# One core, two transformer blocks: a bank wait split in two, three short chains moved, and evacuations spread over the chunks of the next group

## The chip, the cores and the metric

The kernel is one program on one core of one Trainium2 chip. Its five engines run their own instruction lists and meet through semaphores: PE (TensorE, with PEld for its weight loads), DVE (VectorE), ACT (ScalarE), POOL (GpSimd, hardly used here) and SP (SyncE, which issues the DMAs). The metric is the device time of one execution in microseconds (us), lower is better.

## The reference

Two blocks of two layers each run one after the other on 256 rows of width 1024, all in float32. The first block mixes four kinds of attention; the second has an mLSTM layer and an MLA layer, each with a gated convolutional feed-forward. What the change touches is inside these lines:

```python
# first block, each layer (attention = 28 "units" of the kernel)
proj = h @ w_in[layer]                     # q, k, v of all mixers, gates of the NSA heads
kc = gelu(blocks_of(k_c) @ wk1) @ wk2      # compressed keys, values alike; one short chain
g = sigmoid(gates); lam = exp(..) - exp(..) + lambda_init
# second block, mLSTM input: 256 latent and 256 context rows together
x_m = h @ w_up                             # 1024 -> 2048
x_c = silu(dwconv3(x_m, conv_w, conv_b))   # depthwise, 3 taps along the sequence
# second block, feed-forward (ffn(0): 512 rows, ffn(1): 256 rows)
gate, up = split(h @ w_in, 2)              # 1024 -> 2 x 2816
y = (silu(dwconv3(gate, conv_w, conv_b)) * up) @ w_out
```

## The kernel before

**Linears.** Every large product goes through one stream of *groups*. A group is a set of four output tiles of 128 columns (four "tickets", one PSUM bank of 512 float32 columns each; there are 8 banks), accumulated over K = 8 *chunks* of 128 input rows. Each operand is split in a high part in `fp32r`, a copy made by ACT, and a low part, a subtraction made by DVE. PE then multiplies high by high, high by low and low by high, so a chunk of four tickets is 12 matmuls of 128x512 (L758). Input parts lie in `xs` (ACT L1262, DVE L1717), which has room for two chunks of 512 columns: ACT can make the high part of chunk k when PE has done chunk k-2. Weight parts lie in `ws` (ACT L1238, DVE L1692) and come from 1 MB slots of a ring of two that SP fills; a slot holds four chunks, and its split is two operations of 128x1024 on either engine. `feed_to(q)` puts the splits for chunk q on an engine's list; behind chunks 1 and 5 of such a group it adds the split of the next weight slot. PE waits for a chunk's low part, the last of its operands.

**Evacuation.** When a group is done, its banks are emptied while the next group is multiplied. The Python loop `for k in range(KD)` calls `feed_to(nxt.q0 + k)` and then whatever was hung on that k, so the table of k values is the order on ACT and DVE. In the loop of `m_up` (16 tickets, four groups) a ticket p costs ACT the centre tap of the convolution (`centre_tap`, L1453), a copy of the bank (L1470) and later SiLU (L1474), and costs DVE the two outer taps (`outer_taps`, L1965 and L1967). In `ffn(0)` (11 groups of two gate and two up tickets) a pair p costs ACT one centre tap and two copies (L1588, L1591) and later SiLU (L1596), and costs DVE the outer taps and later the product of gate and up (L2210). In the loop of group 1 ACT also scales the residual at k = 6 and 7 (L1449, L1445). SiLU needs another table on ACT than what runs before, so its first use loads it (ACT_TABLE_LOAD).

**First block.** After the linears `proj` and `nat` of a layer, ACT and DVE empty their banks (ACT L1340, L1343, L1344 for `nat`); PE transposes a hidden row of the compression MLP into the bank `hidT` (L918), and then goes through the units: scores `S` of unit i (L952, L953), one modulation product `ada` (L967), the transposes of the probabilities of unit i-2 or so (L1009) and the output `O` of unit i-3 (L1028). Before unit 0 PE waits until all 8 banks from before `hidT` are free. DVE empties `hidT` (L1820), makes the argument of the gelu (L1824 to L1830), then the lambda and the gates (L1832 to L1840), and only then adds the bias to the logits of unit 0 (L1867, L1869). ACT makes the exponential of the gelu (L1354) ahead of its loop, DVE ends the gelu at i = 1 (L1847 to L1851).

Of the kernel before, what the change touches and what calls it, by code (L numbers as in the profile page):

```python
# [391 lines left out]
def build(nc, tokens, stream, side, params, params1, consts, onehot, out, scratch):  # L392
    with ExitStack() as ctx:
# [330 lines left out]
        def _(pe):  # L724
# [156 lines left out]
            for l in range(DEPTH):  # L881
# [39 lines left out]
                for n in range(N(("hidT", l)) - BANKS + 1, N(("hidT", l)) + 1):  # L921
                    pe.wait_ge(bank_free[n % BANKS], n // BANKS + 1)
                for i in range(NU + 3):
# [72 lines left out]
                    if 0 <= i - 2 < NU:  # L996
# [216 lines left out]
        def _(act_):  # L1213
# [349 lines left out]
            def ffn(l, lo):  # L1563

                groups, per = ((NFF // 2, 2), (6, 4))[l]
                for i in range(groups + 1):
# [4 lines left out]
                    start = int(l == 0 and not last)  # L1571
                    for k in range(KD):
# [19 lines left out]
                        if 2 <= k < 2 + before:  # L1592
                            j = per * (i - 1) + k - 2
# [82 lines left out]
        def _(dve):  # L1676
# [85 lines left out]
            for l in range(DEPTH):  # L1762
# [55 lines left out]
                n = N(("hidT", l))  # L1818
                dve.wait_ge(bank_full[n % BANKS], n // BANKS + 1)
                v.tensor_copy(hid.rearrange("p a b -> p (a b)"), ps(n, 0, 64)).then_inc(bank_free[n % BANKS], 1)  # L1820
                dve.wait_ge(bank_free[n % BANKS], n // BANKS + 1)

                gx = lamp.rearrange("p (a b) -> p a b", a=4)
                v.tensor_tensor(gx, hid, hid[:, :, 15:16].to_broadcast([P, 4, 16]), ALU.add).then_inc(dve_own, 1)  # L1824
                dve.wait_ge(dve_own, own(dve_own))
                v.tensor_tensor(hidg, gx, gx, ALU.mult).then_inc(dve_own, 1)
                dve.wait_ge(dve_own, own(dve_own))
                v.tensor_scalar(hidg, hidg, 0.044715, 1.0, ALU.mult, ALU.add).then_inc(dve_own, 1)
                dve.wait_ge(dve_own, own(dve_own))
                v.tensor_tensor(hidg, hidg, gx, ALU.mult).then_inc(gelu_arg, 1)  # L1830
                dve.wait_ge(lam_exp, seen(lam_exp))
                v.tensor_tensor(lam[:, 4:5], lam[:, 3:4], lam[:, 2:3], ALU.subtract)  # L1832
                v.tensor_scalar(lam[:, 6:7], par_at(("subln", l)), 1.0 - lam_init, None, ALU.mult).then_inc(dve_own, 1)
                dve.wait_ge(dve_own, own(dve_own))
                v.tensor_scalar(lam[:, 5:6], lam[:, 4:5], -lam_init, None, ALU.add)

                dve.wait_ge(gate_exp, seen(gate_exp))
                v.tensor_scalar(lam[:, 16:40], lam[:, 16:40], 1.0, None, ALU.add).then_inc(dve_own, 1)
                dve.wait_ge(dve_own, own(dve_own))
                v.reciprocal(lam[:, 16:40], lam[:, 16:40]).then_inc(dve_own, 1)  # L1840
# [631 lines left out]
```

## Time and profile before

| what | value |
|---|---|
| median of three executions | 2338.24 us (2337.72, 2338.24, 2345.36) |
| the profiled execution's own time | 2337.17 us |
| span of the profiled execution | 2335.3 us, mean granted clock 0.996 |
| PE, PEld, DVE, ACT busy | 96%, 80%, 58%, 51% |
| stretch of `m_up` groups 1 to 3 | 793.50 to 865.20 us |
| stretch of `ffn(0)` groups 1 to 10 | 1565.16 to 1793.28 us |
| first unit of layers 1 and 2 | 89.82 and 463.90 us |

The profiled execution took 1.9 us more than its span, and 1.07 us less than the median. All times of the trace count from the start of the span. A line of the timeline gives the start, the duration, the engine, the source line, the operation, what it writes and reads, and in brackets how long the engine was idle before it and whose end it waited for.

### The profile page before, as it was taken

The numbers are of one execution on the slowest core, as the hardware profiler recorded it, in microseconds if no ns is written. First come the engines' busy times: TensorE is split into PE (matmuls) and PEld (weight loads), VectorE is DVE, ScalarE is ACT, GpSimd is POOL, SyncE is SP. The second block draws the span as 40 slices with busy tenths as digits, with TensorE's granted clock in tenths as the row PEclk, the third lists the DMA queues.
The fourth block names the chain that finished last, engine by engine and source line by source line (L and its number), as shares of the span: only waits on it lengthen the run. The fifth ranks groups of instructions, "written<-read, shape, count | busy, mean of one in ns | idle before, by whom it ended". The sixth has DMA issues, their size and how long they took to land.

```text
span 2335.3 us, 33830 instructions
## 1 busy us (share of the span) xinstructions
PE 2251.0 (96%) x13598; PEld 1859.4 (80%) x13598; DVE 1352.0 (58%) x2258; ACT 1193.7 (51%) x2020; POOL 0.2 (0%) x4
## 2 busy tenths in 40 slices
PE   8999999999999999999999999999999998899998
PEld 8759999857999777787677676867777876668998
DVE  6665655666665655445666654365656345546764
ACT  4656545555554564444344443366655336546764
POOL 0000000000000000000000000000000000000000
PEclk9999999999999999999999999999999999999999
DMA  8864555793455213222122221222222222214542
GB/s 309 326 246 145 183 185 179 289 358 125 170 185 186 91 55 108 91 91 99 63 73 72 72 73 54 91 73 90 91 90 92 107 72 91 90 37 146 184 161 106
DMA packets 45721, 312.31 MB, mean 134 GB/s; under 512 B 4951, under 2 KB 7255, under 8 KB 8580
## 3 DMA queue, kind: packets, MB, share of 16 engines
q1 hardware_dynamic: 45572, 310.20, 36.7%
q8 instruction: 108, 1.77, 0.3%
q14 instruction: 41, 0.34, 0.0%
HBM read 309.11 MB, written 1.07 MB: 133 GB/s over the span
## 4 chain that ended last, share of the span: by engine, by line
PE 83%; DVE 8%; ACT 7%; issue 2%; DMA 0%; ACTq 0%; DVEq 0%; SPq 0%
PE bank L758 59%; PE bank L763 8%; DVE ws L1692 3%; ACT ws L1238 2%; PE bank L967 2%; PE bank L1129 1%; DVE xs L1717 1%; PE bank L1028 1%; PE bank L1100 1%; PE bank L953 1%; PE bank L831 1%; PE bank L952 1%; PE bank L1009 1%; PE bank L1191 1%; ACT xs L1262 1%
## 5 line engine op out<-in xcount | busy, mean ns | idle before, releaser
L758 PE MATMUL bank<-xs,ws 128*128 128x256 f32 (+1 forms) x9648 | 1567.1, 324 | 40.7 <-DVE xs L1717 30.7
L758 PEld LDWEIGHTS bank<-xs,ws 128*128 128x128 f32 x9648 | 1400.0, 191 | 209.8 <-DVE xs L1717 46.4
L1692 DVE TENSOR_TENSOR ws<-ring,ws 128x1024 fp32r<-128x1024 f32 x464 | 547.8, 1222 | 279.3 <-ACT ws L1238 279.1
L1238 ACT ACTIVATE ws<-ring 128x1024 fp32r<-128x1024 f32 x464 | 464.7, 1050 | 281.6 <-PE bank L758 273.8
L1717 DVE TENSOR_TENSOR xs<-arena,xs 128x512 fp32r<-128x512 f32 (+1 forms) x286 | 162.4, 581 | 302.4 <-ACT xs L1262 301.2
L1262 ACT ACTIVATE xs<-arena 128x512 fp32r<-128x512 f32 (+1 forms) x286 | 149.2, 539 | 338.7 <-PE bank L758 226.8
L1717 DVE TENSOR_TENSOR xs<-hT,xs 128x512 fp32r<-128x512 f32 (+1 forms) x216 | 133.0, 619 | 178.5 <-ACT xs L1262 178.4
L763 PE MATMUL bank<-ws,xs 128*128 128x512 f32 (+1 forms) x1008 | 228.5, 386 | 6.3 <-ACT arena L1499 2.2
L1262 ACT ACTIVATE xs<-hT 128x512 fp32r<-128x512 f32 (+1 forms) x216 | 122.9, 575 | 199.0 <-PE bank L758 190.3
L763 PEld LDWEIGHTS bank<-ws,xs 128*128 128x128 f32 x1008 | 187.3, 188 | 46.3 <-DVE xs L1717 3.2
L1714 DVE SCALAR_TENSOR_TENSOR xs<-xT,par,xs 128x256 fp32r<-128x256 f32 x112 | 51.2, 480 | 11.9 <-ACT xs L1260 11.9
L1260 ACT ACTIVATE xs<-xT,par 128x256 fp32r<-128x256 f32 x112 | 51.8, 495 | 6.8 <-DVE xT L1732 6.8
L831 PE MATMUL bank<-con 128*128 128x256 f32 x210 | 49.4, 388 | 2.2 <-DVE arena L2229 2.2
L967 PE MATMUL bank<-arena,cs 128*32 128x256 f32 x768 | 51.4, 385 | 0.0
L831 PEld LDWEIGHTS bank<-con 128*128 128x128 f32 x210 | 40.3, 194 | 11.2 <-issue 6.0
L1453 ACT ACTIVATE arena<-bank,par 128x512 f32<-128x512 f32 (+1 forms) x60 | 41.8, 697 | 11.1 <-PE bank L758 11.1
L1272 ACT ACTIVATE arena<-xT 128x512 f32<-128x512 f32 (+1 forms) x52 | 28.5, 562 | 36.4 <-DVE xT L2155 26.6
L1876 DVE SCALAR_TENSOR_TENSOR arena<-bank,arena 128x384 f32<-128x384 f32 x40 | 22.3, 558 | 41.2 <-PE bank L953 41.2
L1377 ACT ACTIVATE arena<-arena 128x128 f32<-128x128 f32 x40 | 16.1, 402 | 58.4 <-DVE arena L1879 58.4
L1129 PE MATMUL bank<-arena 128*128 128x512 f32 (+1 forms) x128 | 42.7, 488 | 0.1
L1965 DVE SCALAR_TENSOR_TENSOR arena<-arena,par 128x510 f32<-128x510 f32 (+1 forms) x60 | 38.9, 648 | 3.3 <-ACT arena L1470 3.3
L1967 DVE SCALAR_TENSOR_TENSOR arena<-arena,par 128x510 f32<-128x510 f32 (+1 forms) x60 | 39.2, 653 | 2.1
(263 smaller groups left out, 1472.4 us busy)
## 6 DMA issues: line engine op xcount, KB each, us to landing
ring<-in_stream SPq DMA_DIRECT2D x233, 1024.0 KB, 4.8
arena<-in_side SPq DMA_DIRECT2D x56, 1024.0 KB, 6.7
arena<-bias_vectors SPq DMA_DIRECT2D x1, 1536.0 KB, 9.1
hT<-in_tokens SPq DMA_DIRECT2D x1, 1024.0 KB, 5.4
arena<-in_tokens SPq DMA_DIRECT2D x1, 1024.0 KB, 12.9
out<-arena SPq DMA_DIRECT2D x2, 512.0 KB, 3.1
arena<-in_params SPq DMA_DIRECT2D x1, 918.0 KB, 8.5
arena<-bias_vectors SPq DMA_DIRECT2D x1, 706.0 KB, 10.6
```

Source lines behind the costliest of these rows:

```text
L758: ins = mm(ps(n, c, c + g.T), a[wi][:, p * P:(p + 1) * P], x[xi], start=first, stop=last)
L763: ins = mm(ps(n, 0, width), x[xi][:, (p // nh) * P:(p // nh + 1) * P], a[wi][:, (p % nh) * 512:(p % nh) * 512 + width], start=first, stop= ...
L831: mm(ps(n, at, at + cols), ones, con[:, 0:cols], start=True, stop=True)
L967: ins = mm(bank[n % BANKS][c:c + 32, 0:T], cs[:, k, 2 * ADA_B - 2 - 2 * u:2 * ADA_B + 30 - 2 * u], wd[:, k, :], start=(u == 0 and k < 4), ...
L1129: ins = mm(ps(n, T_AT[st_], T2), mv[:, st_, h * T2 + e * P:h * T2 + (e + 1) * P], mP[:, 0, OFF[st_]:OFF[st_] + T2 - T_AT[st_]], start=(st_ ...
L1238: do(ws[:, i % 2, 0, c], ring[:, w % R, c], ACT.Copy).then_inc(w_high, 1)
L1260: do(split_x(q, 0), source(g, k), ACT.Identity, scale=par_at(g.gain, k)).then_inc(x_high, 1)
L1262: do(split_x(q, 0), source(g, k), ACT.Copy).then_inc(x_high, 1)
L1453: return do(dst, ps(n, 0, cols), ACT.Identity, scale=w[:, 1:2], bias=b)
L1692: ins = v.tensor_tensor(ws[:, i % 2, 1, c], ring[:, w % R, c], ws[:, i % 2, 0, c].bitcast(F32), ALU.subtract)
L1714: stt(split_x(q, 1), source(g, k), par_at(g.gain, k), split_x(q, 0).bitcast(F32), ALU.mult, ALU.subtract).then_inc(x_done, 1)
L1717: v.tensor_tensor(split_x(q, 1), source(g, k), split_x(q, 0).bitcast(F32), ALU.subtract).then_inc(x_done, 1)
```

## The change

1. PE waits before unit 0 only for the four banks of the last `proj` tickets; for the four banks of `nat` it waits at i = 3, ahead of the first `O`.
2. On DVE the copy of `hidT` and the gelu argument go behind the logits of unit 0, the lambda and the gates behind those of unit 1, and the end of the gelu from i = 1 to i = 2. On ACT the exponential of the gelu goes from ahead of the loop to i = 1.
3. In `m_up` groups 1 to 3 ACT empties one ticket at each of k = 1 to 4 (two at each of k = 1 and 2 before), SiLU goes from k = 2..5 to 3..6, DVE's taps from k = 1..4 to 2..5.
4. In `ffn(0)` groups 1 to 10 ACT's taps and copies go from k = 1, 2 to 2, 3, SiLU from 2, 3 to 4, 5, DVE's taps from 1, 2 to 3, 4 and its products from 3, 4 to 5, 6. The last loop, and `ffn(1)`, keep their order.
5. `silu_tables()`, a table load with no work behind it, stands at the end of the loop i = 0 of `m_up` and of both `ffn`.

```diff
@@ PE, ahead of the units and in their loop
-                for n in range(N(("hidT", l)) - BANKS + 1, N(("hidT", l)) + 1):
+                for n in range(N(("proj", l, 1)), N(("proj", l, 1)) + 4):
                     pe.wait_ge(bank_free[n % BANKS], n // BANKS + 1)
                 for i in range(NU + 3):
...
+                    if i == 3:
+                        for n in range(N(("nat", l)), N(("nat", l)) + 4):
+                            pe.wait_ge(bank_free[n % BANKS], n // BANKS + 1)
                     if 0 <= i - 3 < NU:
@@ ACT
+            def silu_tables():
+
+                act_.preload_act_table_set("silu_and_others")
...
-                act_.wait_ge(gelu_arg, l + 1)
-                do(hid, hidg, ACT.Exp, scale=-2.0 * math.sqrt(2.0 / math.pi)).then_inc(gelu_exp, 1)
                 for i in range(NU + 3):
+                    if i == 1:
+                        act_.wait_ge(gelu_arg, l + 1)
+                        do(hid, hidg, ACT.Exp, scale=-2.0 * math.sqrt(2.0 / math.pi)).then_inc(gelu_exp, 1)
@@ ACT, m_up
-                    if i and 1 <= k < 3:
-                        for p in range(2 * k - 2, 2 * k):
+                    if i:
+                        for p in range(4):
+                            if k != (1 + p if i < 4 else 1 + p // 2):
+                                continue
...
-                    if i and 2 <= k < 6:
-                        j = 4 * (i - 1) + k - 2
+                    if i and 0 <= k - (3 if i < 4 else 2) < 4:
+                        j = 4 * (i - 1) + k - (3 if i < 4 else 2)
...
+                if i == 0:
+                    silu_tables()
@@ ACT, ffn
-                    start = int(l == 0 and not last)
+                    start = 2 * int(l == 0 and not last)
...
-                        if 2 <= k < 2 + before:
-                            j = per * (i - 1) + k - 2
+                        if start + 2 <= k < start + 2 + before:
+                            j = per * (i - 1) + k - start - 2
...
+                    if i == 0:
+                        silu_tables()
@@ DVE, first block: the three chains
                 for i in range(NU + 1):
-                    if i == 1:
+                    if i == 2:
                         dve.wait_ge(gelu_exp, l + 1)
...
+                    if i == 0:
+                        n = N(("hidT", l))
+                        dve.wait_ge(bank_full[n % BANKS], n // BANKS + 1)
...
+                    if i == 1:
+                        dve.wait_ge(lam_exp, seen(lam_exp))
...
@@ DVE, m_up
-                    if i and 1 <= k < 5:
-
-                        j = 4 * (i - 1) + k - 1
-                        n = N(("m_up", i - 1), k - 1)
+                    p = k - (2 if i < 4 else 1)
+                    if i and 0 <= p < 4:
+
+                        j = 4 * (i - 1) + p
+                        n = N(("m_up", i - 1), p)
@@ DVE, ffn
+                    start = 2 * int(l == 0 and not last)
                     for k in range(KD):
                         feed_to(nxt.q0 + k)
-                        if 1 <= k < 1 + before:
+                        p = k - start - 1
+                        if 0 <= p < before:
...
-                        if 3 <= k < 3 + before:
+                        p = k - start - 3
+                        if 0 <= p < before:
```

The line numbers move with the edit: ACT L1238, L1262, L1453, L1470, L1474, L1588, L1591, L1596 of before are L1245, L1269, L1461, L1480, L1484, L1600, L1603, L1608 of the change, and DVE L1692, L1717, L1965, L1967, L2210 are L1706, L1731, L1981, L1983, L2230.

On DVE, one loop of `ffn(0)`: the rows from the weight split (`ws`) that follows chunk 1 to the one that follows chunk 5. The `xs` rows between are the low parts of chunks 2, 3, 4 and 5, L1965 and L1967 are a pair of taps, L2210 is a product. Before:

```order
L1692 TENSOR_TENSOR ws<-ring,ws 128x1024 x2
L1965 SCALAR_TENSOR_TENSOR arena<-arena,par 128x2x255
L1967 SCALAR_TENSOR_TENSOR arena<-arena,par 128x2x255
L1717 TENSOR_TENSOR xs<-hT,xs 128x512
L1965 SCALAR_TENSOR_TENSOR arena<-arena,par 128x2x255
L1967 SCALAR_TENSOR_TENSOR arena<-arena,par 128x2x255
L1717 TENSOR_TENSOR xs<-hT,xs 128x512
L2210 TENSOR_TENSOR arena<-arena 128x512
L1717 TENSOR_TENSOR xs<-hT,xs 128x512
L2210 TENSOR_TENSOR arena<-arena 128x512
L1717 TENSOR_TENSOR xs<-hT,xs 128x512
L1692 TENSOR_TENSOR ws<-ring,ws 128x1024 x2
```

With the change, from the same weight split on, up to the second product:

```order
L1706 TENSOR_TENSOR ws<-ring,ws 128x1024 x2
L1731 TENSOR_TENSOR xs<-hT,xs 128x512 x2
L1981 SCALAR_TENSOR_TENSOR arena<-arena,par 128x2x255
L1983 SCALAR_TENSOR_TENSOR arena<-arena,par 128x2x255
L1731 TENSOR_TENSOR xs<-hT,xs 128x512
L1981 SCALAR_TENSOR_TENSOR arena<-arena,par 128x2x255
L1983 SCALAR_TENSOR_TENSOR arena<-arena,par 128x2x255
L1731 TENSOR_TENSOR xs<-hT,xs 128x512
L1706 TENSOR_TENSOR ws<-ring,ws 128x1024 x2
L2230 TENSOR_TENSOR arena<-arena 128x512
L1731 TENSOR_TENSOR xs<-hT,xs 128x512
L2230 TENSOR_TENSOR arena<-arena 128x512
```

The two pairs of taps leave the place between the first weight split and chunk 2 for the places behind chunks 3 and 4, and the first product now stands between the second weight split and the low part of chunk 6.

On DVE, the end of one loop of `m_up` (groups 1 to 3), from the taps of the third ticket on. Before:

```order
L1965 SCALAR_TENSOR_TENSOR arena<-arena,par 128x2x255
L1967 SCALAR_TENSOR_TENSOR arena<-arena,par 128x2x255
L1717 TENSOR_TENSOR xs<-hT,xs 128x512
L1965 SCALAR_TENSOR_TENSOR arena<-arena,par 128x2x255
L1967 SCALAR_TENSOR_TENSOR arena<-arena,par 128x2x255
L1717 TENSOR_TENSOR xs<-hT,xs 128x512
L1692 TENSOR_TENSOR ws<-ring,ws 128x1024 x2
L1717 TENSOR_TENSOR xs<-hT,xs 128x512 x4
L1692 TENSOR_TENSOR ws<-ring,ws 128x1024 x2
```

With the change:

```order
L1981 SCALAR_TENSOR_TENSOR arena<-arena,par 128x2x255
L1983 SCALAR_TENSOR_TENSOR arena<-arena,par 128x2x255
L1731 TENSOR_TENSOR xs<-hT,xs 128x512
L1981 SCALAR_TENSOR_TENSOR arena<-arena,par 128x2x255
L1983 SCALAR_TENSOR_TENSOR arena<-arena,par 128x2x255
L1731 TENSOR_TENSOR xs<-hT,xs 128x512
L1706 TENSOR_TENSOR ws<-ring,ws 128x1024 x2
L1981 SCALAR_TENSOR_TENSOR arena<-arena,par 128x2x255
L1983 SCALAR_TENSOR_TENSOR arena<-arena,par 128x2x255
L1731 TENSOR_TENSOR xs<-hT,xs 128x512 x4
```

The taps of the last ticket, which stood ahead of chunk 5, now stand behind the weight split that follows chunk 5, so ahead of the low part of chunk 6.

On DVE, the head of the units of a layer, from the copy of `hidT` (128x64) to the logits of unit 0 (128x384). Before:

```order
L1820 COPY arena<-bank 128x64
L1824 TENSOR_TENSOR arena<-arena 128x64
L1826 TENSOR_TENSOR arena<-arena 128x64
L1828 TENSOR_SCALAR arena<-arena 128x64
L1830 TENSOR_TENSOR arena<-arena 128x64
L1832 TENSOR_TENSOR arena<-arena 128x1
L1833 TENSOR_SCALAR arena<-par 128x1
L1835 TENSOR_SCALAR arena<-arena 128x1
L1838 TENSOR_SCALAR arena<-arena 128x24
L1840 RECIPROCAL arena<-arena 128x24
L1867 SCALAR_TENSOR_TENSOR arena<-bank,arena 128x384
L1869 TENSOR_SCALAR arena<-arena 128x384
```

With the change:

```order
L1856 SCALAR_TENSOR_TENSOR arena<-bank,arena 128x384
L1858 TENSOR_SCALAR arena<-arena 128x384
L1873 COPY arena<-bank 128x64
L1877 TENSOR_TENSOR arena<-arena 128x64
L1879 TENSOR_TENSOR arena<-arena 128x64
L1881 TENSOR_SCALAR arena<-arena 128x64
L1883 TENSOR_TENSOR arena<-arena 128x64
L1856 SCALAR_TENSOR_TENSOR arena<-bank,arena 128x384
```

The logits of unit 0 now stand ahead of the copy of `hidT` and its chain of four.

## Rows read from the trace of the kernel before

The granted clock is the number behind the POOL column in the rows of the windows.

**Rows 1.** Waits over the whole run: us in total, times, longest us.
```profile
PE bank L758 <- DVE xs L1717: 30.7, 34, 3.5
PE bank L952 <- ACT arena L1344: 2.0, 2, 1.0
```

**Rows 2.** Windows: span, busy us of PE, PEld, DVE, ACT, POOL, clock, DMA, GB/s.
```profile
793.50:865.20 71.70, 67.16 (x290) 53.60 (x289) 44.68 (x58) 50.27 (x76) 0.00 (x0) 1.00 0.21 74
1565.16:1793.28 228.12, 221.17 (x962) 179.30 (x960) 140.38 (x180) 138.95 (x212) 0.00 (x0) 1.00 0.26 93
```

**Rows 3.** Timeline of PE in the `ffn(0)` groups 0 to 10: start, duration, line.
```profile
1559.59 11.18 PE L758 MATMUL bank<-xs,ws 128*128 128x512 f32 x48
1571.44 3.06 PE L758 MATMUL bank<-xs,ws 128*128 128x512 f32 x12 [0.68 <-DVE xs L1717]
1574.93 19.64 PE L758 MATMUL bank<-xs,ws 128*128 128x512 f32 x84 [0.43 <-DVE xs L1717]
1617.67 22.05 PE L758 MATMUL bank<-xs,ws 128*128 128x512 f32 x96 [0.68 <-DVE xs L1717]
1776.81 19.58 PE L758 MATMUL bank<-xs,ws 128*128 128x512 f32 x85 [0.68 <-DVE xs L1717]
```

**Rows 4.** Timeline of ACT and DVE in the loop of `ffn(0)` group 3.
```profile
1613.20 2.36 DVE L1692 TENSOR_TENSOR ws<-ring,ws 128x1024 fp32r<-128x1024 f32 x2 [0.26 <-ACT ws L1238]
1615.48 0.75 DVE L1965 SCALAR_TENSOR_TENSOR arena<-arena,par 128x510 f32<-128x510 f32 x1
1616.93 0.69 DVE L1717 TENSOR_TENSOR xs<-hT,xs 128x512 fp32r<-128x512 f32 x1
1623.44 0.63 ACT L1262 ACTIVATE xs<-hT 128x512 fp32r<-128x512 f32 x1 [2.09 <-PE bank L758]
1625.06 2.36 DVE L1692 TENSOR_TENSOR ws<-ring,ws 128x1024 fp32r<-128x1024 f32 x2 [0.26 <-ACT ws L1238]
1627.34 0.69 DVE L1717 TENSOR_TENSOR xs<-hT,xs 128x512 fp32r<-128x512 f32 x1
1628.88 0.63 ACT L1262 ACTIVATE xs<-hT 128x512 fp32r<-128x512 f32 x1 [2.09 <-PE bank L758]
```

**Rows 5.** Timeline of DVE around one product, `ffn(0)` group 1.
```profile
1574.79 0.68 DVE L2210 TENSOR_TENSOR arena<-arena 128x512 f32<-128x512 f32 x1
1575.40 0.69 DVE L1717 TENSOR_TENSOR xs<-hT,xs 128x512 fp32r<-128x512 f32 x1
```

**Rows 6.** Timeline around a chunk whose low part came just on time.
```profile
1556.81 9.42 PE L758 MATMUL bank<-xs,ws 128*128 128x512 f32 x40
1558.85 0.68 DVE L1717 TENSOR_TENSOR xs<-hT,xs 128x512 fp32r<-128x512 f32 x1
1565.36 0.63 ACT L1262 ACTIVATE xs<-hT 128x512 fp32r<-128x512 f32 x1 [2.09 <-PE bank L758]
```

**Rows 7.** Timeline of PE in the `m_up` groups 1 to 3, and ACT there.
```profile
799.84 3.03 PE L758 MATMUL bank<-xs,ws 128*128 128x512 f32 x12 [0.73 <-DVE xs L1717]
801.38 1.28 ACT L1474 ACT_TABLE_LOAD   x1
804.61 19.33 PE L758 MATMUL bank<-xs,ws 128*128 128x512 f32 x84 [1.74 <-DVE xs L1717]
811.13 1.90 ACT L1449 ACTIVATE xT<-xT 128x2048 f32<-128x2048 f32 x1
828.01 19.34 PE L758 MATMUL bank<-xs,ws 128*128 128x512 f32 x84 [0.32 <-DVE xs L1717]
848.08 3.06 PE L758 MATMUL bank<-xs,ws 128*128 128x512 f32 x12 [0.73 <-DVE xs L1717]
```

**Rows 8.** Timeline of the first layer's first unit, PE and ACT.
```profile
88.42 0.42 PE L918 MATMUL bank<-con,arena 16*128 16x16 f32 x4
88.95 0.40 ACT L1344 ACTIVATE arena<-bank,arena 128x140 f32<-128x140 f32 x1
89.82 0.46 PE L952 MATMUL bank<-arena 64*128 64x128 f32 x2 [0.98 <-ACT arena L1344]
```

More of the change, by code:

```diff
@@ L1817, in _ @@
                 ins.then_inc(bank_free[n % BANKS], 1)
[L1818 to L1840, printed above, removed]
-                dve.wait_ge(dve_own, own(dve_own))
-                gates = lam[:, 16:40].rearrange("p (a b) -> p a b", a=2)
                 dve.wait_ge(cbias_ready, 1)
                 for i in range(NU + 1):
-                    if i == 1:
+                    if i == 2:
                         dve.wait_ge(gelu_exp, l + 1)
@@ L1880, in _ @@
                                             ).then_inc(logits_ready, 1)
+                    if i == 0:
+                        n = N(("hidT", l))
+                        dve.wait_ge(bank_full[n % BANKS], n // BANKS + 1)
+                        v.tensor_copy(hid.rearrange("p a b -> p (a b)"), ps(n, 0, 64)).then_inc(bank_free[n % BANKS], 1)
+                        dve.wait_ge(bank_free[n % BANKS], n // BANKS + 1)
+                        gx = lamp.rearrange("p (a b) -> p a b", a=4)
+                        v.tensor_tensor(gx, hid, hid[:, :, 15:16].to_broadcast([P, 4, 16]), ALU.add).then_inc(dve_own, 1)
+                        dve.wait_ge(dve_own, own(dve_own))
+                        v.tensor_tensor(hidg, gx, gx, ALU.mult).then_inc(dve_own, 1)
+                        dve.wait_ge(dve_own, own(dve_own))
+                        v.tensor_scalar(hidg, hidg, 0.044715, 1.0, ALU.mult, ALU.add).then_inc(dve_own, 1)
+                        dve.wait_ge(dve_own, own(dve_own))
+                        v.tensor_tensor(hidg, hidg, gx, ALU.mult).then_inc(gelu_arg, 1)
+                    if i == 1:
+                        dve.wait_ge(lam_exp, seen(lam_exp))
+                        v.tensor_tensor(lam[:, 4:5], lam[:, 3:4], lam[:, 2:3], ALU.subtract)
+                        v.tensor_scalar(lam[:, 6:7], par_at(("subln", l)), 1.0 - lam_init, None, ALU.mult).then_inc(dve_own, 1)
+                        dve.wait_ge(dve_own, own(dve_own))
+                        v.tensor_scalar(lam[:, 5:6], lam[:, 4:5], -lam_init, None, ALU.add)
+                        dve.wait_ge(gate_exp, seen(gate_exp))
+                        v.tensor_scalar(lam[:, 16:40], lam[:, 16:40], 1.0, None, ALU.add).then_inc(dve_own, 1)
+                        dve.wait_ge(dve_own, own(dve_own))
+                        v.reciprocal(lam[:, 16:40], lam[:, 16:40]).then_inc(dve_own, 1)
+                        dve.wait_ge(dve_own, own(dve_own))
+                        gates = lam[:, 16:40].rearrange("p (a b) -> p a b", a=2)
                     if i >= 1:
@@ L2195, in ffn @@
                     before = G("ffn_in", l, i - 1).tickets // 2 if i else 0
+                    start = 2 * int(l == 0 and not last)
                     for k in range(KD):
                         feed_to(nxt.q0 + k)
-                        if 1 <= k < 1 + before:
-                            j = per * (i - 1) + k - 1
-                            n = N(G("ffn_in", l, i - 1).name) + (k - 1 if l else 2 * (k - 1))
+                        p = k - start - 1
+                        if 0 <= p < before:
+                            j = per * (i - 1) + p
+                            n = N(G("ffn_in", l, i - 1).name) + (p if l else 2 * p)
                             raw = fup[:, j % 4, 0:T] if l else graw[:, j % 4, :]
@@ L2204, in ffn @@
                             outer_taps(ctmp[:, j % 4, lo:], raw, par_at(("fconv_w", l), 3 * j, 3), len(segs))
-                        if 3 <= k < 3 + before:
-                            j = per * (i - 1) + k - 3
-                            n = N(G("ffn_in", l, i - 1).name) + (k - 3 if l else 2 * (k - 3) + 1)
+                        p = k - start - 3
+                        if 0 <= p < before:
+                            j = per * (i - 1) + p
+                            n = N(G("ffn_in", l, i - 1).name) + (p if l else 2 * p + 1)
                             dve.wait_ge(act_silu, seen(act_silu))
```

## The prediction

> **What bounds the kernel now.** I read four views in this order. The page first: PE is busy 96% of the span at full clock, so only PE's remaining idle time can be won. The waits of PE next: the largest part of it is PE waiting for the low part of a chunk, 30.7 us in 34 waits, and beside it two waits of about 1.0 us, one per layer, for the last `nat` bank [rows 1]. Then the windows, to see which of these lie in the touched stretches: `ffn(0)` groups 1 to 10 take 228.12 us, `m_up` groups 1 to 3 take 71.70, both at clock 1.00 [rows 2]. Last the timelines of PE, ACT and DVE there.
>
> The unit of both stretches is a chunk of 12 matmuls. ACT's high parts are released by PE chunk by chunk, two of them are 5.44 apart (1623.44, 1628.88) [rows 4], so a chunk is 2.72 us and a group of eight 21.76. Such a high part starts 0.20 after PE begins a chunk: group 1 begins at 1565.16 [rows 2], ACT follows at 1565.36 [rows 6]. Ten ffn groups without a wait would take 217.6, so **10.5 us are lost there**; 24 `m_up` chunks would take 65.3, so **6.4 us are lost** there.
>
> Where in a group? PE stops once per ffn group, at chunk 2: seven periods lie between the restarts at 1617.67 and 1776.81 [rows 3], 22.73 each, so the stop costs 0.97. In group 1 the chunk was due at 1565.16 + 5.44 = 1570.60 and began at 1571.44 [rows 3], 0.84 late; the other 0.13 of the 0.97 is the restart itself. The cause is on DVE in group 3 [rows 4]: the weights' low part ends at 1615.56, then stands a pair of taps (1615.48 to 1616.93), and only then the low part of chunk 2, which ends at 1617.62; PE goes on at 1617.67. Nine stops like that are 8.7; the second stop in group 1 (1574.93, 0.8 late) and small ones make up the rest.
>
> In `m_up` it is the same stop in each of three groups (due 793.50 + 5.44 = 798.94, begun 799.84: 0.90 late), plus one at chunk 3: 804.61 instead of 802.56, 2.05 late, behind the table load of 1.28 us on ACT (801.38), and 0.6 late in groups 2 and 3 (828.01 against 824.67 + 2.72) [rows 7]. 3 x (0.90 + 0.13) + 2.05 + 2 x 0.6 is 6.3 of the 6.4.
>
> **The change part by part.**
>
> *ffn(0), chunk 2.* With the taps gone from in front of it, its low part follows the weights: 1615.48 to 1616.17 in group 3, due at 1617.67 - 0.84 = 1616.83, so 0.66 early. That such a margin costs nothing is seen at chunk 6 of the same group, which stands like that today: weights to 1627.42, low part to 1628.03, due at 1628.88 - 0.20 = 1628.68, and PE runs 96 matmuls through it [rows 3, 4]. All ten stops and the one at 1574.93 go: the 10.5.
>
> *ffn(0), chunk 6.* Here the first product now lies between the weights and the low part. A product moves what follows by 0.61 (1574.79 to 1575.40) [rows 5], so chunk 6's low part ends at 1628.64, 0.04 early. What a margin of nothing costs is shown once: chunk 6 of ffn group 0 was due at 1556.81 + 2.72 = 1559.53, and its low part ended at 1558.85 + 0.68 = 1559.53 [rows 6]; PE stopped, restarted at 1559.59 [rows 3] and reached the next group at 1565.16 instead of 1564.97: 0.19. So 0.04 early costs some 0.15, in ten groups 1.5. The bounds are 0 and 0.97 per group, the price of a chunk as late as chunk 2 is now.
>
> A rule of the Trainium skill speaks against this place: "VectorE: DVE Perf Modes", section "The DRAIN you can't avoid", has the next DVE operation start only behind a flush of about the operation's duration less 0.27 us. By an estimate from it chunk 6 would be 0.4 late, the half-late rival below. The same section lets an operation that is not held start earlier, and the row here has the next low part starting 0.07 before the product's end [rows 5]; so the sum goes by the row.
>
> *ffn(0), the rest.* The taps now stand behind the low parts of chunks 3 and 4. In those chunks DVE has a low part (0.69) and a pair of taps (1.45) in 2.72 us, with no weights to split. SiLU is asked for one chunk ahead of its product. I add 0.45 for the residual scaling on ACT in group 1, by the `m_up` estimate below. Loss after: 1.95; **gain 8.55**.
>
> *m_up.* ACT now empties one ticket per chunk, so the high part of chunk 3 no longer stands behind four bank reads, and the table load moves to the end of group 0's loop, where ACT waits for PE about 2 us per chunk. All present stops go (6.4). But the taps of the last ticket now stand behind the second weight split, in front of chunk 6. Chunk 6 stands there today with 0.65 to spare, as in ffn; 1.45 of taps make it 0.80 late, and with the 0.19 above that is 1.0 per group, **three new stops, 3.0**. Bounds: 0, if DVE gets to the taps earlier, and 1.0. In group 1 the last SiLU moves to k = 6, next to the residual scaling of 1.90 us (811.13) [rows 7]: with a high part of 0.63 and a SiLU of about as much ACT has 3.16 in a chunk of 2.72, so about 0.45 late. Loss after 3.45; **gain 2.95**.
>
> *First block.* The transposes of `hidT` end at 88.84, the last `nat` eviction at 89.35, and the scores begin at 89.82 [rows 8]. PE needs only some 0.1 for the four banks that it still waits for, so unit 0 starts at about 88.95, 0.87 earlier. The four waits that move cost PE time again at i = 3: the 0.47 from the eviction's end to the scores is mostly these, and I take 0.2, half of it, for the rest lies beside matmuls still running. 0.67 per layer, two layers: **gain 1.35** (bounds 0, if the softmax of unit 0 or 1 is late instead, and 1.75). The chains on DVE move behind logits that are wanted first; nothing of them is wanted before the compressed keys at i = 4. That hides them; if it didn't, PE would wait at i = 4 for the chain's end, about 1 us a layer.
>
> *The table loads.* Their number stays; each of the three lands in a wait of ACT for PE. In `m_up` its price is in the 6.4, elsewhere it is 0.
>
> **Sum.** 8.55 + 2.95 + 1.35 = 12.85. The profiled execution took 2337.17 us, so 2324.3 for it; the median of the runs lies 1.07 higher, so **2325.4** for the median.
>
> **The rivals.** All in terms of the median.
> - *Half-late product:* chunk 6 of ffn(0) is 0.42 late, half as late as chunk 2 today, so 0.61 a group instead of 0.15: 4.6 more, **2330.0**. For it: a margin of 0.04 is less than any row resolves; and the flush. Against it: the overlap [rows 5].
> - *Full product:* the stop only moves from chunk 2 to chunk 6, 0.97 a group, 8.2 more: **2333.6**, no change by a measurement that tells 0.3% (7.0 us). It needs 0.8 more in front of chunk 6, such as both products; the order puts one there.
> - *m_up keeps its gain:* chunk 6 does not wait, 3.0 less: **2322.4**. It needs taps 0.8 earlier than the weight split lets DVE do them; the order speaks against it.
> - *Slower, late evictions:* ACT's second pair of ffn copies comes late and the taps stand in front of chunk 4 too, so chunks 4 and 6 both stop, 2 x 0.97 a group, nearly 10 us more than today's single stop: **2344** to 2346. It decides when the first taps end 1.8 later than they should: a high part starts 0.20 after PE's chunk and takes 0.63, a low part 0.69, so chunk 3's low part ends 1.52 into chunk 2, the taps 1.45 later or 0.25 into chunk 3, and chunk 4's low part can begin 0.83 into chunk 3 and be done 1.2 early; 0.58 and 1.2 are spare. ACT is busy 139 of 228 us there [rows 2], so I see nothing that would hold it so long.
> - *The stall only changes its name:* what PE no longer waits for in the three places it waits for elsewhere, **2338**. Against it: in these stretches the weights, the banks and DMA have never ended a wait of PE.
>
> **How the numbers follow.** Forecast 0.66; its own range, with chunk 6 of ffn at 0 to 0.3 a group and the first block at 0 to 1.75, is 2323.5 to 2328. Half-late 0.09, full 0.06, `m_up` keeps 0.10, slower 0.04 (half of it beyond 0.3%), same stall 0.05. Faster by over 0.3% means below 2331.2: 0.66 + 0.09 + 0.10 = 0.85, less a little for what nobody listed: 0.84. Slower 0.03, the rest 0.13 within. The range from 2321.0 to 2331.0 takes in the forecast, the half-late case and the case below it.
>
> **What would show it.** In ffn(0) no stop of PE at chunk 2, and stops of at most 0.1 at chunk 6 (ten rows of up to 96 matmuls; if wrong, 0.4 or 0.7 idle there behind DVE L1731). In `m_up` no stop at chunks 2 and 3, three of 0.6 to 0.75 at chunk 6 with L1983 right in front of L1731. The first scores 0.8 to 0.9 earlier after the `hidT` transposes, with no new wait above 0.3 up to i = 4. The prediction is wrong if PE's waits for DVE in the stretch 1565 to 1793 stay above 4 us, or if the units of the first block lose what the first score wins.

## The result and the profile after

The changed kernel takes 2320.85 us in the median of four executions (2318.97 to 2322.40), beside 2337.98 of the kernel before: ratio 0.9919 (0.9898 to 0.9941), 17 us faster. The forecast was 2325.4 with a range from 2321.0 to 2331.0: the right way, in the right places, and 0.15 us outside at the low end. The profiled execution took 2322.40, 14.8 less than that of before; the other 2.4 us of the 17 are the first thing to explain. One execution of a variant further below (the `m_up` part alone) took 3041.86 us at a granted clock of 0.684; it is left out of every median, ratio and fit.

The page of the changed kernel: span, and busy time of each engine.

```profile
span 2320.5 us, 33832 instructions
PE 2246.3 (97%) x13598; PEld 1857.8 (80%) x13598; DVE 1352.5 (58%) x2258; ACT 1194.1 (51%) x2020; POOL 0.2 (0%) x4
```

The waits of PE over the whole run (us in total, times, longest):

```profile
PE bank L758 <- DVE xs L1731: 20.7, 19, 3.5
```

10.0 us less than before [rows 1]; the two waits for the last `nat` bank are gone from the list. The windows of the two stretches, with the columns of [rows 2]:

```profile
792.61:860.24 67.63, 66.22 (x289) 53.82 (x288) 44.76 (x58) 48.90 (x75) 0.00 (x0) 1.00 0.23 78
1561.73:1781.01 219.28, 219.16 (x961) 179.33 (x960) 141.11 (x180) 137.95 (x211) 0.00 (x0) 1.00 0.27 96
```

`m_up` groups 1 to 3 went from 71.70 to 67.63, a gain of 4.1; `ffn(0)` groups 1 to 10 from 228.12 to 219.28, a gain of 8.8. Without any wait they would take 65.3 and 217.6, so 2.35 and 1.7 are still lost. PE's timeline says where. In `ffn(0)` one row covers all the groups of [rows 3]; in `m_up` PE stops twice:

```profile
1545.05 265.16 PE L758 MATMUL bank<-xs,ws 128*128 128x512 f32 x1160 [0.45 <-DVE xs L1731]
```

```profile
787.01 22.08 PE L758 MATMUL bank<-xs,ws 128*128 128x512 f32 x96 [0.48 <-DVE xs L1731]
809.77 22.45 PE L758 MATMUL bank<-xs,ws 128*128 128x512 f32 x96 [0.68 <-DVE xs L1731]
832.89 27.51 PE L758 MATMUL bank<-xs,ws 128*128 128x512 f32 x120 [0.68 <-DVE xs L1731]
```

Group 1 of `m_up` begins at 792.61, so 809.77 is its chunk 6, and 832.89 that of group 2. Group 3 has no stop: the row from 832.89 runs 120 matmuls, ten chunks, to the end of the stage. On DVE around the first of them:

```profile
805.30 2.36 DVE L1706 TENSOR_TENSOR ws<-ring,ws 128x1024 fp32r<-128x1024 f32 x2 [0.26 <-ACT ws L1245]
807.58 0.74 DVE L1981 SCALAR_TENSOR_TENSOR arena<-arena,par 128x510 f32<-128x510 f32 x1
808.36 0.75 DVE L1983 SCALAR_TENSOR_TENSOR arena<-arena,par 128x510 f32<-128x510 f32 x1
809.03 0.68 DVE L1731 TENSOR_TENSOR xs<-hT,xs 128x512 fp32r<-128x512 f32 x1
```

The taps of the last ticket (L1981, L1983) lie between the weight split and the low part of chunk 6, as forecast. In group 3 there is no weight split in front of them; the taps end at 852.36, and the low part of chunk 6 then still waits 0.58 for ACT:

```profile
850.83 0.74 DVE L1981 SCALAR_TENSOR_TENSOR arena<-arena,par 128x510 f32<-128x510 f32 x1
851.61 0.75 DVE L1983 SCALAR_TENSOR_TENSOR arena<-arena,par 128x510 f32<-128x510 f32 x1
852.94 0.69 DVE L1731 TENSOR_TENSOR xs<-hT,xs 128x512 fp32r<-128x512 f32 x1 [0.58 <-ACT xs L1269]
```

In `ffn(0)`, chunk 6 of one group, on DVE, PEld and ACT:

```profile
1618.59 2.36 DVE L1706 TENSOR_TENSOR ws<-ring,ws 128x1024 fp32r<-128x1024 f32 x2 [0.26 <-ACT ws L1245]
1620.87 0.68 DVE L2230 TENSOR_TENSOR arena<-arena 128x512 f32<-128x512 f32 x1
1621.47 0.68 DVE L1731 TENSOR_TENSOR xs<-hT,xs 128x512 fp32r<-128x512 f32 x1
1622.20 0.76 PEld L758 LDWEIGHTS bank<-xs,ws 128*128 128x128 f32 x4 [0.25 <-DVE xs L1731]
1622.41 0.63 ACT L1269 ACTIVATE xs<-hT 128x512 fp32r<-128x512 f32 x1 [1.87 <-PE bank L758]
```

The product (L2230) moves the low part by 0.60, to an end at 1622.15. The next weight load starts at 1622.20 after a wait of 0.25, and PE's timeline makes no break there: a low part that comes at the last moment. The groups repeat every 21.89 us (219.28 less the 0.5 that stays when no product stands there, as shown below, divided by ten, is 21.88) instead of 21.76, so this costs 0.12 each; 0.15 were forecast.

The first unit of layer 1, as in [rows 8]:

```profile
89.21 0.42 PE L918 MATMUL bank<-con,arena 16*128 16x16 f32 x4
89.56 0.49 PE L952 MATMUL bank<-arena 64*128 64x128 f32 x2
89.75 0.40 ACT L1351 ACTIVATE arena<-bank,arena 128x140 f32<-128x140 f32 x1
90.59 0.56 DVE L1856 SCALAR_TENSOR_TENSOR arena<-bank,arena 128x384 f32<-128x384 f32 x1 [5.19 <-PE bank L953]
```

The scores start 0.35 after the transposes of `hidT` start, where it was 1.40, and before the last `nat` eviction (89.75). That is 1.05 for layer 1. In layer 2 it is the same 0.35 after 1.40, and from the first scores of layer 1 to those of layer 2 the kernel is 1.02 shorter (89.56 to 462.62, where it was 89.82 to 463.90).

### The profile page after: what moved, and what is told of

The parts are those of the page before. It is cut to its first block, busy times and chain, and to the rows that moved or that the text cites. A ratio compares the mean times of both kernels' runs of the same rounds, so it can differ in the third digit from the quotient of the medians.

```text
span 2320.5 us, 33832 instructions
## 1 busy us (share of the span) xinstructions
PE 2246.3 (97%) x13598; PEld 1857.8 (80%) x13598; DVE 1352.5 (58%) x2258; ACT 1194.1 (51%) x2020; POOL 0.2 (0%) x4
## 3 DMA queue, kind: packets, MB, share of 16 engines
HBM read 309.11 MB, written 1.07 MB: 134 GB/s over the span
## 4 chain that ended last, share of the span: by engine, by line
PE 87%; DVE 7%; ACT 5%; issue 1%; DMA 0%; ACTq 0%; DVEq 0%; SPq 0%
PE bank L758 62%; PE bank L763 8%; DVE ws L1706 2%; PE bank L967 2%; ACT ws L1245 2%; PE bank L1132 1%; PE bank L1031 1%; PE bank L1103 1%; DVE xs L1731 1%; PE bank L953 1%; PE bank L952 1%; PE bank L1009 1%; PE bank L831 1%; PE bank L1194 1%; PE bank L1065 1%
## 5 line engine op out<-in xcount | busy, mean ns | idle before, releaser
L1706 DVE TENSOR_TENSOR ws<-ring,ws 128x1024 fp32r<-128x1024 f32 x464 | 547.7, 1222 | 277.2 <-ACT ws L1245 277.0
L1245 ACT ACTIVATE ws<-ring 128x1024 fp32r<-128x1024 f32 x464 | 464.7, 1050 | 279.9 <-PE bank L758 272.1
L1731 DVE TENSOR_TENSOR xs<-arena,xs 128x512 fp32r<-128x512 f32 (+1 forms) x286 | 162.4, 581 | 304.0 <-ACT xs L1269 302.9
L1269 ACT ACTIVATE xs<-arena 128x512 fp32r<-128x512 f32 (+1 forms) x286 | 149.2, 539 | 340.3 <-PE bank L758 226.8
L1731 DVE TENSOR_TENSOR xs<-hT,xs 128x512 fp32r<-128x512 f32 (+1 forms) x216 | 133.0, 619 | 164.5 <-ACT xs L1269 164.4
L1269 ACT ACTIVATE xs<-hT 128x512 fp32r<-128x512 f32 (+1 forms) x216 | 122.4, 573 | 187.0 <-PE bank L758 177.7
L1461 ACT ACTIVATE arena<-bank,par 128x512 f32<-128x512 f32 (+1 forms) x60 | 41.5, 692 | 9.9 <-PE bank L758 9.9
L1385 ACT ACTIVATE arena<-arena 128x128 f32<-128x128 f32 x40 | 16.1, 402 | 58.3 <-DVE arena L1868 58.3
L1981 DVE SCALAR_TENSOR_TENSOR arena<-arena,par 128x510 f32<-128x510 f32 (+1 forms) x60 | 38.8, 647 | 3.3 <-ACT arena L1480 3.3
L1983 DVE SCALAR_TENSOR_TENSOR arena<-arena,par 128x510 f32<-128x510 f32 (+1 forms) x60 | 39.1, 652 | 2.1
```

Source lines behind the costliest of these rows:

```text
L1245: do(ws[:, i % 2, 0, c], ring[:, w % R, c], ACT.Copy).then_inc(w_high, 1)
L1269: do(split_x(q, 0), source(g, k), ACT.Copy).then_inc(x_high, 1)
L1461: return do(dst, ps(n, 0, cols), ACT.Identity, scale=w[:, 1:2], bias=b)
L1706: ins = v.tensor_tensor(ws[:, i % 2, 1, c], ring[:, w % R, c], ws[:, i % 2, 0, c].bitcast(F32), ALU.subtract)
L1731: v.tensor_tensor(split_x(q, 1), source(g, k), split_x(q, 0).bitcast(F32), ALU.subtract).then_inc(x_done, 1)
```

## The experiments

**Reading times at one clock.** Each execution comes with its mean granted clock, to 0.001. Over the 117 executions of all kernels of this study whose clock is known (41 of before, 14 of the changed one) one straight line fits: a level for each kernel, and 1.75 us (1.63 to 1.87) for each 0.001 of clock, with 0.8 us left over. Below, "at one clock" is the difference of two such levels, with its 95% interval. The differences of medians are given beside it.

| kernel | median us | ratio to before | at one clock, against before |
|---|---|---|---|
| changed kernel, second time | 2321.39 | 0.9931 (0.9918 to 0.9944) | -15.1 +- 0.5 (all three times) |
| changed kernel, third time | 2322.08 | 0.9940 (0.9926 to 0.9953) | |
| first block's part alone | 2334.35 | 0.9985 (0.9976 to 0.9994) | -2.05 +- 0.5 |
| `m_up` part alone | 2333.91 | 0.9982 (0.9971 to 0.9993) | -4.4 +- 0.5 |
| `ffn(0)` part alone | 2328.06 | 0.9957 (0.9945 to 0.9970) | -9.2 +- 0.8 |
| last `m_up` taps later | 2317.74 | 0.9917 (0.9903 to 0.9930) | -17.5 +- 0.8 |
| `ffn(0)` products later | 2319.62 | 0.9927 (0.9913 to 0.9941) | -16.6 +- 0.8 |
| both products at k = 5 | 2327.59 | 0.9957 (0.9943 to 0.9970) | -9.9 +- 0.8 |
| both later | 2320.83 | 0.9928 (0.9914 to 0.9941) | -18.5 +- 0.6 (both times) |
| both later, again | 2317.53 | 0.9926 (0.9912 to 0.9940) | |
| bank waits split, chains not moved | 2319.68 | 0.9927 (0.9913 to 0.9940) | -16.1 +- 0.8 |
| no preload in `m_up` | 2323.28 | 0.9941 (0.9927 to 0.9954) | -14.3 +- 0.8 |

Kernels were run in three batches, the third of them on another chip; before had medians of 2338.32, 2336.27 and 2335.09 in them. Each variant has line numbers of its own, a few off those of the changed kernel. Lengths of stretches below are from the traces, from the first matmul of group 1 to the first one behind the last group.

| kernel | `m_up` groups 1 to 3 | `ffn(0)` groups 1 to 10 |
|---|---|---|
| before | 71.69 | 228.12 |
| changed | 67.63 | 219.28 |
| `m_up` part alone | 67.61 | 228.17 |
| `ffn(0)` part alone | 71.74 | 219.32 |
| last `m_up` taps later | 65.28 | 219.37 |
| `ffn(0)` products later | 67.64 | 218.14 |
| both products at k = 5 | 67.64 | 225.33 |
| both later, again | 65.28 | 218.13 |
| no preload in `m_up` | 67.99 | 219.22 |

**The changed kernel again, and its three parts alone.** The parts are the edits 1 and 2, 3, and 4 of the section on the change, each with its preload, put into the kernel before.

> The changed kernel once more, beside before on one chip. Theory 1 (terms that were sized too small, and a spread between executions on top): 14 to 15 us faster than before in the median of more executions, that is 2323 to 2324 where before has 2338, with single executions 1 to 2 us to either side. Theory 2 (all 17 us are the work of the change, and the profiled execution was a slow one): 17 us again, 2321, and its executions lie closer together than 1 us around it.

> Only the first block's part (bank waits split, chains moved). Theory 1: the first scores of each layer 1.03 earlier and no new wait behind them, 2.0 us faster than before. The prediction's own term was 1.35. A rival, that the waits at i = 3 or the later gelu give some back, has 1.0 or less.

> Only the m_up part with its table preload. Theory 1: chunks 2 and 3 run through in all three groups, chunk 6 stops in groups 1 and 2 (0.96 each) and not in group 3, where no weight split follows chunk 5, and chunk 7 of group 1 0.4 late: 3.9 us faster. The prediction's term was 2.95, with three stops at chunk 6.

> Only the ffn(0) part, with the preloads of both ffn stages. Theory 1: each of ten groups loses 0.97 at chunk 2 less and 0.12 at chunk 6 more, with the second stop of group 1 gone: 8.9 us faster. The prediction's term was 8.55. If the three parts together don't reach what the changed kernel gains in the same call within 1.5 us, the parts help each other or the spread between executions is the rest.

The median of the changed kernel was 2321.39, its executions from 2319.4 to 2323.3: the median of theory 2 with the spread of theory 1. The granted clocks bring them together: at one clock the gain is 15.1, near theory 1, and most of what the medians show beyond it goes with the clock (in this batch 0.9966 in the mean of the changed kernel and 0.9958 of before, 1.4 us by the line). Of the first four executions of the changed kernel one had 0.998 and three 0.997. The parts are worth 2.05, 4.4 and 9.2, together 15.6, so they neither help nor hinder each other. The stretches of each part alone are the same as in the whole, to 0.1.

Of the first block's 2 x 1.04 not all stays. Where the second block's first linear starts, PE waits for nothing that the profile shows, 0.47 in the kernel before, 0.81 in this part alone:

```profile
768.70 2.51 PE L758 MATMUL bank<-xs,ws 128*128 128x512 f32 x10 [0.81 <-issue]
```

It is the same 0.81 in the changed kernel. So by the trace the part is worth 2.07 - 0.34 = 1.7; the 2.05 +- 0.5 at one clock holds either.

**Taps and products one chunk later.** The edits to the changed kernel, DVE's lines (ACT's SiLU follows in `m_up`):

```diff
-                    p = k - (2 if i < 4 else 1)
+                    p = {2: 0, 3: 1, 4: 2, 6: 3}.get(k, -1) if i < 4 else k - 1
```

```diff
-                        p = k - start - 3
+                        p = k - start - 3 - start // 2
```

> The changed kernel with the last ticket's taps in m_up groups 1 to 3 one chunk later (k = 6, SiLU at k = 7), so that no taps stand between a weight split and the low part of chunk 6. Theory: the two stops at chunk 6 (0.68 idle, 0.96 with the restart, groups 1 and 2) go, 1.9 us faster than the changed kernel at the same clock, so 17.2 under before where the changed kernel is 15.3 under. A rival, that the weight split itself makes chunk 6 late, leaves the stops and the time. If the residual scaling now meets the SiLU of chunk 7 in group 1, 0.4 of it comes back.

> The changed kernel with the products of ffn(0) groups 1 to 10 one chunk later (k = 6 and 7), so that none stands in front of the low part of chunk 6. Theory: chunk 6 has its 0.65 of margin again and the 0.12 per group go, 1.2 us faster than the changed kernel at the same clock. A rival, that the 0.12 in each group is something else than the late low part, leaves a group period of 21.89 instead of 21.76.

PE of the first variant runs through the three groups in one row, 312 matmuls from chunk 6 of group 0 to the end:

```profile
786.12 71.01 PE L758 MATMUL bank<-xs,ws 128*128 128x512 f32 x312 [0.47 <-DVE xs L1732]
```

65.28 is 24 chunks of 2.72 without any loss: the two stops and the 0.4 of group 1 are gone, 2.35 by the stretches, 2.4 +- 0.8 at one clock. That the 0.4 goes too says what it was. In the changed kernel, on ACT, DVE and PEld at chunk 7 of group 1:

```profile
809.14 0.63 ACT L1484 ACTIVATE arena<-arena 128x512 f32<-128x512 f32 x1 [1.89 <-DVE arena L1983]
809.68 1.90 ACT L1457 ACTIVATE xT<-xT 128x2048 f32<-128x2048 f32 x1
811.49 0.61 ACT L1269 ACTIVATE xs<-hT 128x512 fp32r<-128x512 f32 x1
812.13 0.69 DVE L1731 TENSOR_TENSOR xs<-hT,xs 128x512 fp32r<-128x512 f32 x1 [2.42 <-ACT xs L1269]
812.87 3.28 PEld L758 LDWEIGHTS bank<-xs,ws 128*128 128x128 f32 x15 [0.48 <-DVE xs L1731]
```

SiLU waits 1.89 for the late taps, the residual scaling (L1457) stands behind it, and the high part of chunk 7 behind that. With the last taps later, high part, SiLU and scaling stand in one chunk just the same, and PE does not stop:

```profile
808.21 0.63 ACT L1269 ACTIVATE xs<-hT 128x512 fp32r<-128x512 f32 x1
808.84 0.63 ACT L1485 ACTIVATE arena<-arena 128x512 f32<-128x512 f32 x1
809.37 1.90 ACT L1457 ACTIVATE xT<-xT 128x2048 f32<-128x2048 f32 x1
```

With the products later the ffn groups lose 218.14 - 217.60 = 0.5 in all instead of 1.7; 1.1 by the stretch, 1.5 +- 0.8 at one clock. Both theories hold: what stood between a weight split and a low part cost what the arithmetic said. The 0.5 that stays lies at the end of group 1, behind the residual scaling there.

**Both products in front of chunk 6.** The loop over pairs in the changed kernel, with both at k = 5 in the ten groups:

```diff
-                        p = k - start - 3
-                        if 0 <= p < before:
+                        for p in range(before):
+                            if k != start + 3 + (0 if start else p):
+                                continue
```

> The changed kernel with both products of ffn(0) groups 1 to 10 at k = 5, so that two stand in front of the low part of chunk 6: the prediction's full-product rival, made on purpose. Theory: the second product moves the low part by 0.61 as the first did, 0.57 late, which with the 0.19 of a chunk just on time is 0.76 a group instead of 0.12, so 6.4 us slower than the changed kernel. If a flush stood behind each product, chunk 6 would be some 0.4 or 0.8 later still, 10 to 14 us slower. If a weight split's margin were larger than reckoned, under 3.

On PE and on DVE:

```profile
1622.84 22.10 PE L758 MATMUL bank<-xs,ws 128*128 128x512 f32 x96 [0.44 <-DVE xs L1731]
1645.37 22.09 PE L758 MATMUL bank<-xs,ws 128*128 128x512 f32 x96 [0.44 <-DVE xs L1731]
```

```profile
1618.61 2.36 DVE L1706 TENSOR_TENSOR ws<-ring,ws 128x1024 fp32r<-128x1024 f32 x2 [0.26 <-ACT ws L1245]
1620.89 1.29 DVE L2231 TENSOR_TENSOR arena<-arena 128x512 f32<-128x512 f32 x2
1622.09 0.69 DVE L1731 TENSOR_TENSOR xs<-hT,xs 128x512 fp32r<-128x512 f32 x1
```

The two products take 1.29 together, the low part starts 0.09 before the second one's end, and the stop is 0.44 in each group. Groups repeat every 22.53, 0.64 more than in the changed kernel; 0.76 - 0.12 was the theory's. The flush that the Trainium skill tells of ("VectorE: DVE Perf Modes", "The DRAIN you can't avoid") does not stand behind a product here; the same section's exception, that an operation which is not held starts earlier, is what this trace shows. The stretch is 6.05 longer, and at one clock the kernel 5.25 +- 0.8 slower than the changed one. The prediction's "full product" rival was priced too high, at 0.97: it would have been 0.77 (22.53 - 21.76).

**Both later.**

> The last taps of m_up and the products of ffn(0) both one chunk later. Theory: the two gains add up, 3.1 us faster than the changed kernel at the same clock, 18.4 under before; its executions differ by the granted clock, 1.8 us for each 0.001.

> The variant with the last taps of m_up and the products of ffn(0) one chunk later, once more. Its clock was 0.9952 in its first executions; if that was chance, it comes to 0.996 or 0.997 here and its median to 3 us under the changed kernel, near 2318. If the variant itself lowers the clock, 2321 again.

At one clock it is 18.5 +- 0.6 under before, and 3.4 +- 0.7 under the changed kernel, as the sum of the two. The first time its clock was 0.994 to 0.996 and its median 2320.83, no better than the changed kernel; the second time, on the other chip, the clock was 0.997 in four of five and the median 2317.53, beside 2322.08 of the changed kernel in the same batch. The program is the same, so the low clock does not belong to the variant. At one clock this is the fastest version that was run.

**The bank waits without the chains.** The changed kernel with the hidT copy, the gelu, the lambda and the gates back where they were. On DVE (ACT's exponential likewise):

```diff
+                n = N(("hidT", l))
...
                 for i in range(NU + 1):
-                    if i == 2:
+                    if i == 1:
                         dve.wait_ge(gelu_exp, l + 1)
...
-                    if i == 0:
-                        n = N(("hidT", l))
...
-                    if i == 1:
-                        dve.wait_ge(lam_exp, seen(lam_exp))
```

> The changed kernel with the three chains of the first block where they were before; only the bank waits are split there. Theory 1: the scores of unit 0 still start 1.0 earlier, but its logits stand behind the chains on DVE and come a microsecond later than in the changed kernel, and what is waiting for the probabilities on PE gives half of it back: 0.5 a layer, 1 us slower than the changed kernel at the same clock. Theory 2, the chains were off the path: the same time within 0.5.

Theory 1 falls. The scores start as early as in the changed kernel, the logits of unit 0 begin 2.12 behind them (91.39 and 89.27) where the changed kernel has 1.03 (90.59 and 89.56), and PE loses nothing by it:

```profile
88.92 0.42 PE L918 MATMUL bank<-con,arena 16*128 16x16 f32 x4
89.27 0.48 PE L952 MATMUL bank<-arena 64*128 64x128 f32 x2
91.39 0.56 DVE L1880 SCALAR_TENSOR_TENSOR arena<-bank,arena 128x384 f32<-128x384 f32 x1
100.55 0.65 PE L1031 MATMUL bank<-arena 128*64 128x256 f32 x2
```

From the first scores to the first output `O` (L1031) it takes 11.28 us. In the changed kernel it takes 11.27, from 89.56 to

```profile
100.83 0.65 PE L1031 MATMUL bank<-arena 128*64 128x256 f32 x2
```

The time is even 1.0 +- 0.8 lower at one clock. The trace has 0.34 of it, the wait at the second block's first linear for which the profile shows no reason, 0.47 here as before:

```profile
768.63 2.75 PE L758 MATMUL bank<-xs,ws 128*128 128x512 f32 x11 [0.47 <-issue]
```

So the chains were off PE's path through the units at either place, the whole gain of the first block is the four bank waits, and moving the chains costs 0.34 at this row. DVE is where the 0.34 comes in: ahead of its first low part of that linear it is idle for 0.72 in the changed kernel (first row) and for 0.38 here (second row), and the high part from ACT had ended 0.46 before in the one and 0.11 in the other:

```profile
768.46 0.69 DVE L1731 TENSOR_TENSOR xs<-hT,xs 128x512 fp32r<-128x512 f32 x1 [0.72 <-ACT xs L1269]
767.84 0.69 DVE L1730 TENSOR_TENSOR xs<-hT,xs 128x512 fp32r<-128x512 f32 x1 [0.38 <-ACT xs L1269]
```

Why DVE starts it later with the chains moved, 680 us before, no run shows.

**Without the preload.** In the `m_up` loop of the changed kernel:

```diff
-                if i == 0:
-                    silu_tables()
```

> The changed kernel without the table preload in m_up, so that the first SiLU loads the table at k = 3 of group 1. Theory 1: in the new order the load of 1.28 makes ACT's chunk 3 about 3.9 long (high part 0.63, tap 0.76, copy 0.59, load 1.28, SiLU 0.63), the next high part 1.2 late, and a low part has 1.2 to spare when nothing else stands before it: no more than 0.3 slower than the changed kernel. Theory 2: the stop of 2.05 at chunk 3 before was the load's, and comes back at chunk 4: 1.5 to 2 slower.

On ACT and on PE:

```profile
799.16 1.28 ACT L1484 ACT_TABLE_LOAD   x1
```

```profile
809.24 22.45 PE L758 MATMUL bank<-xs,ws 128*128 128x512 f32 x96 [1.04 <-DVE xs L1729]
```

The load of 1.28 comes back, in chunk 2 of group 1, and there is no stop at chunk 3 or 4. What it moves reaches chunk 6, which waits 1.04 instead of 0.68: 0.36 by the stretch, 0.8 +- 0.8 at one clock. Theory 2 falls. Before, chunk 3 lost 2.05 in group 1, with the load, and 0.6 in groups 2 and 3, without it [rows 7]. So the load seems to have cost its length only behind taps and copies two by two, which no run separates; once these are spread it costs 0.36.

**The clock.**

> The changed kernel a third time, for its granted clock. If the change takes away stretches at half clock, its executions keep a higher mean clock than those of before, 0.9969 against 0.9960 so far, 1.6 us; if that was chance, the means come together and the difference of the medians goes from 17 towards the 15.2 at one clock.

The means come together: 0.9967 and 0.9962. In this batch the medians are 13.0 us apart (2335.09 and 2322.08), in the first comparison 17.1. It is the same pair of programs. Whether the change moves the mean clock a little is not settled by 0.0005 (0.9 us); the last section has a place where it could.

## Why the prediction missed

The forecast was 12.85 us by the profiled execution. Measured in the traces, it is 4.06 + 8.84 + 1.7 = 14.6, and 15.1 +- 0.5 at one clock. By steps:

- **ffn(0), chunk 2** held: all stops there and the one of 1574.93 are gone. (Of the two pairs of taps only the first stood ahead of chunk 2 before, as the order shows; the second stood behind it.)
- **ffn(0), chunk 6** held: 0.15 forecast, 0.12 measured, with the product at the place and the length that [rows 5] gave. Gain 8.84 against 8.55; the residual scaling in group 1 took 0.5, where 0.45 were forecast. That the sum went by the row of the product and by no pause behind it was right, shown again with two products.
- **m_up, the step that failed:** "three new stops, 3.0". There are two. The piece of order that it rested on was one loop; in the loop of group 3 no weight split follows chunk 5, since the stage behind it takes its weights from the ring unsplit (L1065), so the taps there delay nothing. That is 1.0 of the 1.1 by which the term (2.95, measured 4.06) was short. The two stops that there are cost about 1.0 each, as forecast. The 0.45 for the last SiLU and the residual scaling came out in size (0.4) by luck: it was reckoned as three jobs too long for one chunk, and those three in one chunk cost nothing with the taps later; what cost it was SiLU waiting 1.89 for taps that stood behind the weight split.
- **First block:** the mechanism was right, the size was not. Neither the 0.1 for the four banks ahead of unit 0 nor the 0.2 for the four at i = 3 shows in the trace: the scores start before the transposes end (89.56, and 89.21 + 0.42), and from there to the first `O` it is 11.27 us, where it was 11.24 (89.82 to 101.06). So 1.04 a layer instead of 0.67. The term's reason for moving the chains, that the logits are wanted first, was not needed, and the move costs 0.34 elsewhere. 1.7 against 1.35.
- **The table load** held as 0 at its new place.
- **From the profiled execution to the median:** the forecast added 1.07. Which clock the executions would have had no place in the sum or in the range. By the line, 2.0 of the 17.1 us were that; the changed kernel's executions had 0.997 to 0.998, those of before in that comparison are not known, so this share is argued and not shown. It took both to cross the low end: with the clock alone the median would have been 2337.98 - 12.85 - 2.0 = 2323.1, with the larger gain alone 2337.98 - 15.1 = 2322.9, both inside.

The rivals: half-late and full product did not come, and the experiment with both products shows what the full one would have cost. That `m_up` keeps its gain came by a third, in group 3, from a cause that the rival did not name. Late evictions did not come: no stop at chunk 4 in any group. Nor did the stall change its name: the time fell by more than the 10.0 us that PE waits less for low parts.

## What to carry to other kernels

Where one engine prepares operands just ahead of another, write down for each chunk what stands on its list between the longest job (here a weight split) and the next due operand; a few tenths of margin decide, and durations from one trace predict them to 0.1 us. Check such a list for every loop, the last one above all, not for one of them. And compare two kernels at one clock before asking where a few microseconds went.

## What was not expected of the hardware

The granted clock falls to 0.50, the lower level of 1.2 GHz, at a handful of places, mostly for 3.4 us, and whether it does at a given place differs from one execution to the next of the same code. Windows of the kernel before, and of the changed one:

```profile
1953.80:1960.60 6.80, 6.17 (x29) 6.17 (x30) 2.32 (x6) 2.27 (x4) 0.00 (x0) 0.50 0.37 147
2240.50:2243.90 3.40, 3.31 (x15) 3.31 (x16) 3.29 (x10) 1.90 (x6) 0.00 (x0) 0.50 0.79 299
```

```profile
933.00:936.40 3.40, 3.40 (x10) 2.62 (x9) 0.69 (x1) 0.63 (x1) 0.00 (x0) 0.51 0.69 289
1941.50:1948.30 6.80, 6.07 (x36) 5.86 (x36) 3.24 (x7) 3.01 (x6) 0.00 (x0) 0.75 0.36 147
2227.00:2230.40 3.40, 3.23 (x26) 3.23 (x27) 3.29 (x10) 1.99 (x6) 0.00 (x0) 1.00 0.83 304
```

Clock is the number behind POOL. At the same piece of code before had 0.50 over 6.8 us where the changed kernel had 0.75 (1953.80 and 1941.50), and 0.50 where that had 1.00 (2240.50 and 2227.00). The other way round, the changed kernel has 0.51 from 933.00, after a wait of PE of 2.18 us, and before has the same wait and no fall behind it:

```profile
932.04 6.21 PE L763 MATMUL bank<-ws,xs 128*128 128x512 f32 x19 [2.18 <-ACT arena L1511]
```

```profile
936.98 4.40 PE L763 MATMUL bank<-ws,xs 128*128 128x512 f32 x18 [2.18 <-ACT arena L1499]
```

19 matmuls take 6.21 us in the one and 18 take 4.40 in the other. Apart from the end of the program, all 50 falls in the traces of this study begin within 1.6 us of the end of a wait of PE of 1.7 to 3.5 us, at seven places, and no trace has a fall at all seven. Five traces have an eighth such wait, of 1.8 us, and no fall at it. One of the seven is the stop of 1.74 at chunk 3 of `m_up` [rows 7]: in the first block's part alone, which still has it, the clock was 0.50 from 804.20 to 807.60, and the 84 matmuls from there took 20.97 us where before has 19.33:

```profile
803.17 20.97 PE L758 MATMUL bank<-xs,ws 128*128 128x512 f32 x84 [1.76 <-DVE xs L1725]
```

The change removes this stop, so some executions of before may lose 1.6 us there that the changed kernel can't lose. That the spread of the kernel before, 2332.3 to 2345.8 us, is mostly these falls is what the line of 1.75 us for each 0.001 of clock says, with its 0.8 us left over.
